# Four places of one instruction order changed in a hybrid attention and mixture-of-experts step

## The reference, cut to what matters

```
h = rms_norm(x);  z = h @ w_in        # columns: u (512) | q | k | v (1024 each) | gate logits (2048)
ext = concat(pool_buf, u)             # the last 15 rows of ext are returned: new_pool
d = (trailing mean over 2, 4, 8, 16 tokens of ext, by channel group) - u
pool_y = (d @ pool_w per group) * pool_scale
attn = rms_norm((softmax(q1 k1) - lam * softmax(q2 k2)) @ v) * (1 - lam_init)     # 8 heads
merged = sigmoid(gate_A) * (pool_y @ w_pool_branch) + sigmoid(gate_B) * (attn @ w_attn_branch)
x = x + merged @ w_out
x = x + top-2 of 16 SwiGLU experts (rms_norm(x)), then a last rms_norm
```

## Time and profile before

| | |
|---|---|
| time, median of 3 runs | 842.15 us (842.1 to 843.49) |
| the profiled execution, whole | 843.01 us |
| its span, first to last instruction | 841.2 us |
| mean granted TensorE clock | 0.993 |
| TensorE, VectorE, ScalarE, GpSimd busy | 97%, 70%, 61%, 11% of the span |

### The profile page before, as it was taken

The page is one execution under the profiler, slowest core; times in us unless marked ns, Lnnn a source line. Parts: engine busy times, 40 slices in busy tenths (PEclk is TensorE's granted clock), DMA queues, the critical chain, the costliest instruction groups (busy, mean ns, idle before and its releaser), DMA issues.

```text
span 841.2 us, 15813 instructions
## 1 busy us (share of the span) xinstructions
PE 819.5 (97%) x5363; PEld 747.1 (89%) x5363; DVE 589.1 (70%) x957; ACT 512.4 (61%) x935; POOL 88.4 (11%) x77
## 2 busy tenths in 40 slices
PE   9999999999999999999999999999999999999992
PEld 8999999999999998999998888888888888888881
DVE  7383233687778767466457126899989999989995
ACT  7344214567666656554634233588888888888884
POOL 0000000000000000000000001122233322223112
PEclk9999999999999999999999999999999999999997
DMA  8541222233123312332335745799999999999924
GB/s 250 123 146 57 79 68 74 68 109 89 45 81 108 86 44 92 105 99 75 101 101 195 265 165 188 254 371 376 380 375 372 364 371 365 368 366 368 345 69 192
DMA packets 135817, 163.02 MB, mean 194 GB/s; under 512 B 18584, under 2 KB 103704, under 8 KB 135772
## 3 DMA queue, kind: packets, MB, share of 16 engines
q1 hardware_dynamic: 129674, 149.53, 52.7%
q0 software_dynamic: 5952, 12.82, 5.4%
q10 hardware_dynamic: 146, 0.07, 0.0%
HBM read 151.09 MB, written 20.12 MB: 204 GB/s over the span
## 4 chain that ended last, share of the span: by engine, by line
PE 53%; DVE 3%; DMA 2%; issue 1%; ACT 1%; POOLq 0%; POOL 0%; ACTq 0%
PE ps L1767 15%; PE ps L1769 15%; PE ps L1768 15%; PE ps L2219 2%; PE ps L2131 1%; DMA xg<-sum_rows,idi 1%; PE ps L2138 1%; PE ps L2241 1%; DMA sum_rows<-yb,ydn 1%; PE ps L2123 0%; PE ps L2164 0%; PE ps L2165 0%; PE ps L2062 0%; DVE wl L1153 0%; PE ps L1990 0%
## 5 line engine op out<-in xcount | busy, mean ns | idle before, releaser
L1642 DVE TENSOR_TENSOR wl<-rawM,wh 128x1024 fp32r<-128x1024 f32 x189 | 223.9, 1219 | 14.4 <-ACT wh L989 14.2
L989 ACT ACTIVATE wh<-rawM 128x1024 fp32r<-128x1024 f32 x192 | 195.6, 1055 | 6.7 <-PE ps L1769 3.7
L1767 PE MATMUL ps<-hTh,wh 128*128 128x272 f32 (+2 forms) x440 | 129.2, 294 | 1.5 <-ACT qkv L813 1.0
L1769 PE MATMUL ps<-hTh,wl 128*128 128x272 f32 (+2 forms) x440 | 127.4, 290 | 0.0
L1768 PE MATMUL ps<-hTl,wh 128*128 128x272 f32 (+2 forms) x440 | 126.8, 288 | 0.0
L1767 PE MATMUL ps<-wh,xh 128*128 128x256 f32 (+1 forms) x384 | 124.7, 325 | 0.3 <-DVE xl L1688 0.3
L1769 PE MATMUL ps<-wh,xl 128*128 128x256 f32 (+1 forms) x384 | 122.0, 318 | 0.0
L1768 PE MATMUL ps<-wl,xh 128*128 128x256 f32 (+1 forms) x384 | 122.0, 318 | 0.0
L1767 PE MATMUL ps<-wh,hTh 128*128 128x384 f32 x256 | 90.0, 352 | 0.2 <-DVE mA L1273 0.2
L1769 PE MATMUL ps<-wh,hTl 128*128 128x384 f32 x256 | 86.4, 337 | 0.0
L1768 PE MATMUL ps<-wl,hTh 128*128 128x384 f32 x256 | 86.2, 337 | 0.0
(11 more groups left out here) (331 smaller groups left out, 1715.0 us busy)
## 6 DMA issues: line engine op xcount, KB each, us to landing
rawM<-in_w_expert_up SPq DMA_DIRECT2D x64, 512.0 KB, 10.1
rawM<-in_w_expert_down SPq DMA_DIRECT2D x64, 512.0 KB, 8.6
rawM<-in_w_expert_gate SPq DMA_DIRECT2D x64, 512.0 KB, 9.0
rawA<-in_w_in SPq DMA_DIRECT2D x64, 192.0 KB, 3.1
rawA<-in_w_in SPq DMA_DIRECT2D x20, 512.0 KB, 5.3
rawA<-in_w_attn_branch SPq DMA_DIRECT2D x8, 512.0 KB, 3.5
rawA<-in_w_out SPq DMA_DIRECT2D x8, 512.0 KB, 4.3
x<-in_x_prompt SPq DMA_DIRECT2D x4, 512.0 KB, 6.0
```

The source lines that it names most:

```text
L989: nc.scalar.activation(wh[:, (c + 1) % S, :], rawM[:, slot, :], ACT.Copy).then_inc(m_hi, 1)
L1642: V.tensor_tensor(wl[:, sl, :], rawM[:, slot, :], wh[:, sl, :].bitcast(F32), ALU.subtract).then_inc(m_lo, 1)
L1767: T.matmul(out, sh, mh_, start=start, stop=False, **kw)
L1769: return T.matmul(out, sl, mh_, start=False, stop=stop, **kw)
```

## The change

Four orders change, and no instruction is added or removed.

- In the list of jobs `last` goes ahead of gA3 (it becomes j = 7, and gA3 j = 8). All engines and SP follow the list.
- In `first_columns` the four transposes of the old state, with their two waits, go ahead of u0's late products.
- For the last head, VectorE splits chunk GB0+7 behind `probs(7, 2)` and not ahead of it.
- `scaled(1)` goes ahead of the split of chunk AB0, and `scaled(2)` ahead of that of AB0+1.

```
@@ the list of jobs
             if i == 3:
-                jobs.append(("last", 0, []))
+                jobs.insert(len(jobs) - 1, ("last", 0, []))
@@ VectorE, attend
                     probs_lo(g, i - 1)
-                    if last:
+                    if last and i < NGR - 1:
                         nxt(3 + 2 * i)
@@ VectorE, last head
             probs(HEADS - 1, 2, link)
+            split_to(GB0 + 7)
             probs_lo(HEADS - 1, 2)
@@ VectorE, the attention's norm
             scaled(0)
+            scaled(1)
             split_to(AB0)
-            scaled(1)
+            scaled(2)
             split_to(AB0 + 1)
-            scaled(2)
             attention_lo(0)
@@ TensorE, first_columns
                 pe.wait_ge(xt_lo, NT)
-                for k in range(KD):
-                    pool_columns(0, 0, k, 1)
                 pe.wait_ge(cst_in, 16)
                 pe.wait_ge(st_in, 16)
                 for g in range(NG):
                     ins = T.transpose(ps[:, 6, P * g:P * g + BUF], stt[0:BUF, P * g:P * g + P],
                                       cst[0:BUF, C_ID:C_ID + BUF])
                 ins.then_inc(st_mm, 1)
+                for k in range(KD):
+                    pool_columns(0, 0, k, 1)
```

## The result

| | before | changed |
|---|---|---|
| median of 18 runs | 841.92 us | 843.62 us |
| lowest to highest | 841.31 to 843.69 | 841.84 to 845.14 |
| ratio, 95% interval | | 1.0019 (1.0012 to 1.0025) |

That is +1.7 us, inside the range given (841.7 to 844.8) and on the forecast side, but 0.6 us more than the +1.1 of the sum. Two of its terms were wrong and had opposite signs, as the experiments show, so that the number came out near is partly luck. Two disturbed runs of the kernel before (1346 and 2316 us) are left out of all that follows.

A forecast was written before the change was run, and what follows sets the result against it. TensorE's nearly unbroken stream of products (busy 819.5 of 841.2 us) bounds the kernel. The terms, 2.10 + 0 - 0.26 - 0.73 = +1.11 us, put the median at 843.3 us from 842.15; range for 8 in 10, 841.7 to 844.8.

The forecast's parts named there:

- the sum: All four reorderings together: 2.10 + 0 - 0.26 - 0.73 = +1.11 us on the span.
- Edit A, the hole opened and the hole closed: `last` ahead of gA3: 2.63 us new standing before gA3, 0.53 removed ahead of pA0, net 2.10 us later.
- Edit B: Old state's transposes ahead of u0's late products: job 1's u columns end 0.3 to 0.5 us sooner, net taken as 0.
- of the gain 0 to 0.05 us is left: At gA0: TensorE already just waits for chunk 4's low half, so the earlier 0.3 to 0.5 us is lost.
- Rival 3: State transposes' gain survives because chunk 4 lands earlier in an unprofiled execution: +0.7 us, 842.85 us; chance 0.09.
- Edits C and D: Last head's E and second attention tile ahead of chunk splits: gains of 0.26 and 0.73 us (the latter 0.57 to 0.81).
- The second wait behind E: At `turn_probs`: bank 7 must be emptied by ScalarE until 378.03, limiting the gain to 0.26 instead of 0.66 us.
- Rival 2: Late steps behind the moved splits take back the last-head and attention gains: +2.1 us alone, 844.25 us; chance 0.13.
- Rival 4, the clock: TensorE's clock falls to 1.2 GHz in the new hole: about 3.2 us lost, +4.3 in all, 846.5 us; chance 0.04.
- so a hole of this size leaves it at 2.4 GHz: At gA3's hole, 3.5 us without a product: clock stays full, since at the kernel's end it stayed 1.00 through 826 to 830.
- Rival 1, no hole: No hole appears at gA3, so moving `last` only gives -0.53 us: some 840.5 us in all; chance 0.07.

The follow-up runs named there:

- C and D alone: Only E of the last head and the second attention tile put ahead of the chunk splits, against the kernel before: 842.01 against 842.58 us, ratio 0.9985.
- edit A alone: Only `last` put ahead of gA3, against the kernel before: 845.61 against 842.58 us, ratio 1.0031.
- The kernel with the hole filled: Changed kernel plus 11 unread products behind the transposes of `last`; 842.53 against 841.71 us for the kernel before, ratio 1.0011.

## Why the prediction came out as it did

- **Edit A, the hole opened and the hole closed: right.** +2.10 forecast, 55.37 - 53.30 = +2.07 in the changed kernel's first profile, +2.04 alone. That the wait ends with pl1's eviction is shown by moving that eviction: the hole moved with it. That pll and not pst is its last step follows from the code.
- **Edit B: the step "of the gain 0 to 0.05 us is left" failed.** Its size was right (0.38 where I had 0.3 to 0.5), but it is not lost at chunk 4. I took the arrival of one load from a single execution, the one in which ScalarE began on it 2.2 to 3.5 us later than in the 12 later profiles. Rival 3 had 0.09; it is what happens.
- **Edits C and D: right.** 0.99 forecast, 0.98 to 1.1 found, D at the upper end of its bounds (0.82) and C at 0.16 and 0.38. The second wait behind E appeared as forecast, 0.3 us on ScalarE's line 829. Rival 2, that a later step takes the gain back, is excluded up to the experts: from the product behind the second attention tile's transposes to the experts' first product it is 143.02 us before and 143.00 and 142.98 in the two profiles of the changed kernel. The time of C and D alone, 0.4 to 2.1 us faster by its interval, shows that some of it reaches the end. Behind the experts' first product the scatter of 305.1 to 308.0 us hides a shift of one microsecond in a single profile.
- **Rival 4, the clock: the step "so a hole of this size leaves it at 2.4 GHz" failed.** It rested on one stretch at the end of one execution, with nothing behind it that multiplies. The first profile of the changed kernel shows no fall either, and yet it falls in 18 of 27 runs, by the mean clock. I gave this 0.04. Its price was too high, 3.2 us instead of 1.5, because I took the sixteen slow products of the kernel's start for the fall. The profile of before doesn't even list a lower clock there (3 to 6 us, columns as in the earlier trace rows), so those rows couldn't show what a fall costs; why they are 0.42 us apart stays open:

```profile
3.00:6.00 3.00, 3.00 (x9) 2.33 (x8) 0.36 (x2) 2.14 (x6) 0.63 (x1) 1.00 0.96 347
```

- **The sum, corrected:** +2.07 - 0.38 - 1.0 = +0.7, and the clock's 1.5 in two of three runs, +1.0: +1.7 us. The measured +1.7 has an interval of 1.0 to 2.1, so the exact match says little. From the last 256-column product to the product behind the second tile's transposes the traces give +0.5 without the fall and +2.0 with it (366.75 and 368.33 against 366.29 us). Among the first 18 runs the ten of low clock average 844.21 and the others 843.18 us, 1.0 apart instead of 1.5; falls missed by the count would bring them closer.
- **Rival 1, no hole: excluded** by every profile with edit A.
- **Open:** why the clock falls in one execution and not in the next with the same hole. With edit A alone it was low in only 4 of 11 runs, which may be chance. Times 1.5 us that would make up the excess of that kernel (2.6 against 2.04), but its seven other runs average 845.45 us, also 2.6 over the kernel before (842.88), so the clock as counted doesn't account for it.

## What to carry to other kernels

Where consecutive jobs alternate between two halves of PSUM, a tiny job is a bad separator: the one behind it inherits the wait for the one before it, with nothing left to cover the eviction; put small work inside a long job instead. When TensorE would stand for 2.0 to 2.6 us, as here, count a share of executions in which its clock falls, and look at the mean clock of many runs, not at one profile. And don't cost a gain at nothing because one execution's load came late: a load's arrival early in a kernel needs more than one trace.

## What was unexpected of the hardware

- A gap with no product but eight transposes, 2.6 us of it idle, brought TensorE to 1.2 GHz in about two thirds of the runs, and a gap with 2.0 us idle in 8 of 11; in the two traces that show it, it fell 1.1 and 1.2 us after the products had resumed and stayed so for fifteen of them. With five products of 512 columns in the gap, and 1.5 us idle behind them, none of 11 runs had a low mean clock.
- The parts of one kernel that move between executions are its start and its end: the last 256-column product started at 25.1 to 26.2 us, and the stretch from the experts' first product to the end took 305.1 to 308.0 us, while the 143 us ahead of it differed by at most 0.25 us over 13 profiles. The kernel with the hole filled shows it best: its profiled execution took 844.99 us, 2.5 more than its median, with no fall of the clock and 308.0 us in that last stretch.
